# Whole second experts, two or three early down-weight blocks, and the last output columns of the first experts in four pieces

## The reference, cut to what matters

```python
def _ec_moe(h, w_router, w_gate, w_up, w_down):        # first block: 16 experts, 32 tokens each
    cap = EC_FACTOR * L // N_EXPERTS
    vals, idx = lax.top_k(jnp.swapaxes(aff, 1, 2), cap)
    hid = silu(einsum('becd,edf->becf', xs, w_gate)) * einsum('becd,edf->becf', xs, w_up)
    y = einsum('becf,efd->becd', hid, w_down) * vals[..., None]
    return jnp.zeros_like(h).at[bidx, idx].add(y)
# the block ends with x + mod * moe, then _rmsnorm(x, norm_final_g)

def hier_moe(x, ...):                                   # each of the two layers: 4 groups x 8 experts
    g_star = argmax(lg)                                 # one group per token
    top_v, top_i = lax.top_k(le, TOP_K_IN_GROUP)        # two experts of the group per token
    for g in range(N_GROUPS):
        h = silu(einsum('td,edf->tef', t, w_gate[g])) * einsum('td,edf->tef', t, w_up[g])
        y = y + einsum('tef,efd->td', h * gate[:, g, :, None], w_down[g])

def second_block(...):
    for l in range(2):
        mix = hybrid_mixer(x, ...)                      # attention of three kinds
        x = layer_norm(ALPHA * x + mix, ...)
        x = layer_norm(ALPHA * x + hier_moe(x, ...), ...)
```

## Time and profile before

| | us |
|---|---|
| median of 3 runs | 1617.17 (1615.1 to 1618.91) |
| the profiled execution | 1616.84 |
| its span in the trace | 1615.1 |
| TensorE busy | 1344.6 (83%) |
| DMA | 492.62 MB, mean 305 GB/s |
| first experts | about 230 to 701 |
| mixer, layer 0 | about 711 to 923 |
| experts, layer 0 | about 923 to 1151 |
| mixer, layer 1 | about 1159 to 1372 |
| experts, layer 1 | about 1372 to 1601 |

### The profile page before, as it was taken

How to read it: one execution, slowest core, us unless ns; L and a number is a source line. 1 busy time by engine, 2 the same in 40 slices (tenths; PEclk the granted TensorE clock), 3 DMA queues, 4 the chain that set the end, 5 groups by cost and what they waited for, 6 DMA issues and landing times. The chain is left out here.

```text
span 1615.1 us, 18893 instructions
## 1 busy us (share of the span) xinstructions
PE 1344.6 (83%) x7496; PEld 747.6 (46%) x7496; DVE 482.2 (30%) x1128; ACT 297.7 (18%) x617; POOL 0.2 (0%) x4
## 2 busy tenths in 40 slices
PE   6999999956665656599999999866999989998658
PEld 4665877412211211166767743321567677433213
DVE  5125553101101101014664522210246744322102
ACT  2422202100000000012332312200223223122002
POOL 0000000000000000000000000000000000000000
PEclk9999999978878878799999999997999999999889
DMA  9465478999999999992421499999915214899994
GB/s 392 165 253 208 159 292 329 399 428 427 428 428 427 428 428 428 428 425 78 191 105 53 164 396 391 410 409 408 388 53 209 86 71 157 343 401 409 409 407 193
DMA packets 63297, 492.62 MB, mean 305 GB/s; under 512 B 7008, under 2 KB 7392, under 8 KB 39008
## 3 DMA queue, kind: packets, MB, share of 16 engines
q1 hardware_dynamic: 63056, 491.15, 74.9%
q10 hardware_dynamic: 144, 0.13, 0.0%
HBM read 490.21 MB, written 1.05 MB: 304 GB/s over the span
## 5 line engine op out<-in xcount | busy, mean ns | idle before, releaser
L659 PE MATMUL PS<-A 128*128 128x256 f32 (+5 forms) x1568 | 367.5, 392 | 5.3 <-DMA A<-ring_d 1.6
L1015 PE MATMUL PS<-A 128*32 128x512 f32 x1536 | 234.2, 747 | 140.1 <-DMA A<-ring_d 140.1
L659 PEld LDWEIGHTS PS<-A 128*128 128x128 f32 (+1 forms) x1568 | 274.3, 193 | 90.1 <-issue 51.0
L1540 PE MATMUL PS<-A 128*32 128x512 f32 (+1 forms) x1024 | 168.0, 628 | 41.1 <-DMA A<-ranked_d 32.9
L1015 PEld LDWEIGHTS PS<-A 128*32 128x32 f32 x1536 | 52.5, 125 | 308.6 <-issue 239.6
L1569 PE MATMUL PS<-A 128*32 128x512 f32 (+1 forms) x512 | 93.9, 713 | 31.6 <-issue 31.6
L1540 PEld LDWEIGHTS PS<-A 128*32 128x32 f32 (+1 forms) x1024 | 48.1, 123 | 143.9 <-issue 143.3
L2096 DVE TENSOR_TENSOR A<-A,PS 128x512 f32<-128x512 f32 x8 | 5.5, 688 | 322.7 <-PE PS L1015 322.7
L664 PE MATMUL PS<-A 128*128 128x128 f32 (+1 forms) x396 | 58.4, 278 | 18.2 <-DVE A L2096 7.1
L664 PEld LDWEIGHTS PS<-A 128*128 128x128 f32 (+1 forms) x396 | 44.7, 144 | 56.0 <-issue 31.0
L1569 PEld LDWEIGHTS PS<-A 128*32 128x32 f32 (+1 forms) x512 | 25.9, 137 | 96.0 <-issue 95.4
(11 more groups left out here) (392 smaller groups left out, 1277.8 us busy)
## 6 DMA issues: line engine op xcount, KB each, us to landing
A<-ring_d SPq DMA_DIRECT2D x156, 2048.0 KB, 26.3
A<-ranked_d SPq DMA_DIRECT2D x240, 512.0 KB, 14.7
A<-ranked_d SPq DMA_DIRECT2D x24, 1024.0 KB, 8.4
A<-ring_d SPq DMA_DIRECT2D x2, 1312.0 KB, 22.2
A<-ring_d SPq DMA_DIRECT2D x2, 1280.0 KB, 22.4
A<-p_d SPq DMA_DIRECT2D x1, 1232.0 KB, 22.6
A<-xT_d SPq DMA_DIRECT2D x1, 1024.0 KB, 5.3
A<-cT_d SPq DMA_DIRECT2D x1, 1024.0 KB, 11.8
```

Source lines behind the costliest of these rows:

```text
L659: ins = g.matmul(out, l, r, start=n == 0, stop=n == len(pairs) - 1)
L1015: ins = g.matmul(ps[32 * e:32 * e + 32, :], rows_of(kk, e), wv[:, kk % 2, e, :], start=kk == 0, stop=kk == 7)
L1540: ins = g.matmul(ps[m * s:m * s + m, :], XS2[u % 2][:, kk, c:c + m], wv[:, kk % nk, s, :], start=kk == 0, stop=kk == 7)
```

## The change

**1. Whole experts.** A `gr` block is now gate and up of one expert, one DMA of 2 MB; a `dr` block of a unit with four experts holds two experts, 2 DMAs of 1 MB. `gate_up` of units 4 to 10 waits for all of its 2 or 4 blocks, does its matmuls, and frees all slots at its end. SyncE reads the experts' numbers at other places.

**2. Early down blocks.** Three more places for blocks, used once per layer (`ONCE`): slot 12 is `YE2[0]`, a quarter of `XGT` and the arrays `PX2[1]`, `PXG[1]` and `GB1`; slot 13 is half of `XGT` and the place of `YE2[1]`; slot 14 (last layer alone) lies in `Ho` and `ARENA2`. The down blocks of units 0 and 1 (and 2 in the last layer) go there, and are asked for before their turn (`AHEAD`). SyncE waits for the end of the mixer's use of these arrays. The second group's tokens are gathered behind unit 3 instead of units 1 to 3, since they are written where the early blocks lie, and the copy of the first half of `ye2` waits for both halves in units 0 and 1.

**3. The last columns of the first experts.** The last four `w_down` blocks hold 128 columns and all rows each. Each piece is multiplied, copied, combined and squared by itself.

```diff
@@ -92,7 +92,7 @@
     x, j = UNITS[n]
     if x == 0:
-        return [(j // 2 + 1, j % 2)]
+        return [[(1, 0)], [(1, 1)], [], [(2, 0), (2, 1)]][j]
...
-    return {1: (0,), 2: (1,), 4: (0,), 5: (1,)}.get(n, ())
+    return {3: (0, 1), 4: (0,), 5: (1,)}.get(n, ())
...
+AHEAD = [{(2, 1): 0, (3, 1): 1}, {(2, 0): 2, (2, 1): 0, (3, 1): 1}]
...
-IDS_BEHIND = {("gu", 3, 0): range(0, 4), ("gu", 3, 1): range(4, 8), ("dn", 4): range(8, 10)}
+IDS_BEHIND = {("gu", 3, 1): range(0, 2), ("gr", 1, 0, 0): range(2, 4), ("gr", 1, 0, 1): range(4, 6), ("dn", 6): range(6, 10)}
...
-    + [4, 5, 0, 1, 2, LAST_SLOT, 4, 5, 0, 1] + [2, LAST_SLOT, 4, 5, 6, 0, 1] * 6 + [2, LAST_SLOT, 4, 5, 6, 0] \
...
+    + [4, 5, 0, 1, 2, LAST_SLOT, 4, 5, 0, 1] + [2, LAST_SLOT, 4, 5, 6, ONCE, 0, 1, ONCE + 1] + [2, LAST_SLOT, 4, 5, 6, 0, 1] * 5 + [2, LAST_SLOT, 4, 5] \
...
+        RING += [[YE2[0], V(Mo + quarter, quarter), V(behind, half_slot)],
+                 [V(Mo + half_slot, half_slot), V(mem_of_ye1, half_slot)],
+                 [V(Ho, half_slot), V(ARENA2, half_slot)]]
...
+            def last_columns(q):
+
+                w, i = weights("w_down", 3, 1, q)
+                wv = w.rearrange("p (k e n) -> p k e n", k=8, e=4)
+                ps = fresh("ye", 3, 1, q)
+                arrived(i)
+                for kk in range(8):
+                    for e in range(4):
+                        ins = g.matmul(ps[32 * e:32 * e + 32, 0:128], HIDT[:, kk, 32 * e:32 * e + 32], wv[:, kk, e, :], start=kk == 0, stop=kk == 7)
+                ins.then_inc(*full("ye", 3, 1, q))
+                finished(i)
...
+            last_columns(3)
+            squares((6,), 6, "row")
+            keep_on(1, "ye", 3)
+            combine_row(7)
+            keep_on(2, "ex", 3)
+            squares((7,), 7, "row").then_inc(*full("fsum"))
...
+            def whole_experts(n, ps):
+
+                (x, j), u = UNITS[n], gather_of(n)
+                m = 32 if four(n) else 64
+                got = [weights("gr", l, x, j, s) for s in range(128 // m)]
+                wv = [w.rearrange("p (k n) -> p k n", k=8) for w, i in got]
+                for d in range(4):
+                    g.wait_ge(*at("xs2", l, u, d // 2, d % 2))
+                for w, i in got:
+                    arrived(i)
+                for kk in range(8):
+                    for s in range(128 // m):
+                        c = (j % 2) * 128 + s * m
+                        ins = g.matmul(ps[m * s:m * s + m, :], XS2[u % 2][:, kk, c:c + m], wv[s][:, kk, :], start=kk == 0, stop=kk == 7)
+                ins.then_inc(*full("sg", l, n))
+                for w, i in got:
+                    finished(i)
...
-                full("ye2", l, p, 0)
+                full("ye2", l, p, int(p < 2))
...
-                n = SLOT // len(of)
-                c = n * part + (4096 if kind == "dr" else 0)
+                of, n, c = (of[part:part + 1], SLOT, 0) if kind == "gr" else (of[2 * part:2 * part + 2], SLOT // 2, SLOT)
...
+                if SLOTS[i] >= ONCE:
+                    q.wait_ge(*at(*(("full", "pv", key[1], "dil", 3), ("full", "wo", key[1], 3), ("sc", key[1], "dil", 3))[SLOTS[i] - ONCE]))
```

More of the change, by code:

```diff
@@ L1110, in tensor @@
                 g.wait_ge(*at("hidt", x, 1))
-                for half in range(2):
+                for half in range(2 if x < 3 else 1):
                     ps = fresh("ye", x, half)
@@ L1535, in gate_up @@
+                for part in range(2):
+                    if (n, part) in AHEAD[l]:
+                        d = AHEAD[l][n, part]
+                        state["down", d] = weights("dn", l, 2 * d)
+                    w, i = weights("gu", l, n, part)
+                    wv = w.rearrange("p (k s n) -> p k s n", k=4, n=512)
+                    for d in (2 * part, 2 * part + 1):
                         g.wait_ge(*at("xs2", l, u, d // 2, d % 2))
                     arrived(i)
-                    for kk in range(nk * part, nk * part + nk):
-                        for s in range(128 // m):
-                            c = (j % 2) * 128 + s * m
-                            ins = g.matmul(ps[m * s:m * s + m, :], XS2[u % 2][:, kk, c:c + m], wv[:, kk % nk, s, :], start=kk == 0, stop=kk == 7)
@@ L1541, in gate_up @@
-                    ins.then_inc(*(full("sg", l, n) if part == parts_ - 1 else up("pe")))
+                    for kk in range(4 * part, 4 * part + 4):
+                        for s in range(2):
+                            c = (j % 2) * 128 + s * 64
+                            ins = g.matmul(ps[64 * s:64 * s + 64, :], XS2[u % 2][:, kk, c:c + 64], wv[:, kk % 4, s, :], start=kk == 0, stop=kk == 7)
+                    ins.then_inc(*(full("sg", l, n) if part else up("pe")))
+                    finished(i)
@@ L1552, in turned, with down_weights @@
                 turn(ps[:, 256:384], pxg).then_inc(*full("hd", l, p))
+            def down_weights(w):
+                pieces = w if type(w) is list else [w]
+                return [p[:, c:c + SLOT // 4] for p in pieces for c in range(0, p.shape[-1], SLOT // 4)]
             def down(n):
@@ L3293, in sync @@
                     ranked(i, x, *key)
+                elif x >= ONCE:
+                    c = 0
+                    for part in RING[x]:
+                        wide = part.shape[-1]
+                        q.dma_start(part, ring_d[row[i], :, c:c + wide]).then_inc(*land(f"ring{x}", *(("landed", i) if c + wide == n else ())))
+                        c += wide
                 else:
```

98 lines of the change are left out of this document (56 added, 42 removed).

## The result

The changed kernel takes 1611.26 us (median of 20 runs, 1606.06 to 1619.67), the kernel before 1616.98 (20 runs on the same chips, 1613.57 to 1624.11). The ratio is 0.9961, with a 95% interval of 0.9950 to 0.9973: 6.3 us less (4.4 to 8.1). The forecast of 1604 was 13 us less. The direction is right, and less than half of the gain came.

The account below looks back on a forecast made before the run. TensorE bounds each expert stage up to about unit 6, DMA landings from unit 8. Columns -3.2, layer 0 -4.7 and layer 1 -5.1 sum to -13.0 us: 1604 us forecast, range 1597 to 1615.

Parts of the forecast that it names:

- the rate behind it: Expert stage, 27 blocks from unit 4's down block to the last landing: 133.4 us, a gain of about 6.3 per layer.
- rival A: Units 8 to 10: long `gate_up` bursts starve the DMA queue, 10 us more than forecast, 1627 us; chance 10%.
- The lead-in loss: Before unit 6: slots held to `gate_up`'s end make unit 4's down block land 1.7 (layer 0), 2.4 us (layer 1) later.
- my sum: Whole kernel: -3.2 us last columns, -4.7 layer 0, -5.1 layer 1, together -13.0 us.
- Early blocks, nothing: Part 2, before the expert stages: the DMA runs 9.8 and 14.7 us ahead, but slots bind, so nothing is gained.
- The hole about unit 4: Sign that the forecast is right: the DMA idles some 10 us about unit 4 while SyncE waits for `gate_up`.
- Rival B: Expert stages: slots don't bind and the early blocks count in full, giving 1575 us; chance 5%.
- The size of rows: Expert-stage transfers: 16 KB rows move at 428 GB/s against 409, `gr` blocks 4.90 us for 5.13, `dr` blocks 5.0.
- Rival C: Expert-stage transfers: larger rows move no faster when the queue is full, only the columns gain, 1614.5 us; chance 10%.
- The last columns, 3.2 us: Part 3, end of first experts: last landing to root takes 4.2 us for 7.4, and the mixer carries the gain on.
- Bursts: Sign that the forecast is right: bursts of `gate_up` on TensorE take 7 to 10 us.
- the own range: The forecast's own range, 1598 to 1610 us: DMA term -2 to -7 per layer, columns -2 to -4.

Follow-up runs that it names:

- a kernel without held slots: Changed kernel with whole experts only for units 7 to 10, units 4 to 6 in row parts: 1604.18 us; without early blocks 1603.99 us.
- the other order: Changed kernel with each `combine_row` ahead of the next `last_columns`, fewer idle products: 1609.30 us; with whole experts only for units 7 to 10 too: 1603.26 us.
- expert by expert: Changed kernel with each expert's products done one behind another, freeing each slot early: 1706.58 us, 1.0570 of the kernel before; without early blocks 1704.21 us.

## Why the prediction was right or wrong

**The step that failed** is the second of part 1, "the rate behind it: a gain of about 6.3 us per layer". It counted 27 blocks back to back from the landing of unit 4's down block. I had priced held slots at units 4 and 5, and asked whether bursts of units 8 to 10 starve the queue (rival A), where TensorE waits for landings and four free blocks are asked for in time. I didn't ask it of unit 6. This is the first unit of four, it holds four of seven slots, and TensorE isn't waiting there: its `gate_up` starts when TensorE comes to it (1012.14), not when its blocks have landed. So unit 7's third block couldn't be asked for before 1019.4. The term was 6.3 and 6.9 us a layer and measured 3.7 and 3.1 in the trace. Of the 6.4 us that are missing, unit 6's hold is 4.3 (1.7 and 2.6). The rest is mostly one block a layer that was asked for in time and came 1.1 and 1.4 us late, which stays open. With unit 6 in parts alone the 27 blocks take 134.5 / 135.5 us, so 3.2 of the 6.4 come back.

**The lead-in loss** was right in the trace in layer 0 and 0.9 too large in layer 1 (+1.7 and +1.5 us, forecast +1.7 and +2.4). I booked it as a price of the part, so it is no part of the shortfall, but it was avoidable. That units 4 to 6 in parts take 1604.2 us, the very forecast, is luck: that kernel doesn't have the lead-in loss. Without it my sum gives 13.0 + 4.1 = 17.1 us less, 1600, and 15.2 (12.3 to 18.3) were measured.

**Early blocks, nothing:** right, measured alone (0.9994 [0.9983, 1.0005]), beside whole experts (0.9970 with them, 0.9968 without) and in a kernel without held slots (0.9906 with them, 0.9915 without). The hole about unit 4 with SyncE waiting for `gate_up` is there as described. Rival B is out.

**The size of rows:** right as to the rate. Seven slices at 410 to 425, single blocks 4.9 apart, pairs 4.95 for my 5.0, and with four DMAs of 4 KB rows the gain vanishes; that it is the row and not the number of DMAs isn't shown. Rival C is out; the trace of before had the answer, 409 against 428 GB/s.

**The last columns, 3.2 us:** the runs have 3.6 (1.8 to 5.5) alone, and 1.4 on top of the other parts, which their intervals don't tell from none. Both ends of the difference were wrong: before is 7.4 to 9.8 and not 7.4, the new form 6.0 to 9.3 and not 4.2 (5.3 and 6.9 in the other order). The traces show 1.5 us at the root, 0.7 of it at unit 0, where I had let the mixer carry all of it. That the number came out near mine was in part luck. I read a single execution and left TensorE's own readiness out: with the old form its products start with the landing where the length is 7.4, and 2.3 us behind it where it is 9.7 and 9.8.

**Bursts:** 8.4 to 10.0 us, forecast 7 to 10; the last `down` stands at 1149.18 behind a landing at 1149.1, and 1.0 behind in layer 1 (0.6 forecast). Rival A, that bursts behind waits starve the queue, is out: in 1015 to 1140 it moves 418 GB/s. A hold does starve it, at another unit and by another mechanism than a slow clock.

**Slips that change little:** the layer-1 sum takes 7.03 us for a `gate_up` that the earlier trace rows has at 7.09; the terms of the own range (-2 to -7 us a layer, -2 to -4 for the columns) give 1599 to 1611 and not 1598 to 1610; and the earlier trace rows has, beside the 390 to 428 GB/s named for the expert stages, slices at 388 and 343.

## What to carry to other kernels

When a change makes a step take its buffers all at once, walk the ring unit by unit and ask at each whether the consumer starts when the data land or when it comes to them. In the first case the hold was free here, in the second the queue ran dry before the slots came back, 1.7 and 2.6 us for a step of 7.07; so use the large transfers only from the unit on at which the consumer waits. Sum the gain from the last instant at which the queue can be starved, and check which that is after the change, not before. And take a handover of a few microseconds from more than one execution: here the same code gave 7.4 and 9.8, and a mixer in code that is alike 226.1 and 228.4.

## What the runs showed of the hardware

Products of 32 columns overlap when they write different quarters of the output's 128 partitions by turns. The same 64 products of 128 x 512 took 7.07 us by turns on four quarters, 12.25 on two, 22.59 on one, all at a granted clock of 1.00. The Trainium skill (TensorEngine Tiling (Array Packing), Overview) gives up to 4 times, as a theoretical figure, for 32 columns; 22.59 / 7.07 is 3.2. What it costs to reorder such products is seen in expert by expert: 95 us.

A block asked for while another is on its way took longer to land: the third block of unit 7 takes 10.1 us from its issue at 1019.4, where the block ahead of it landed at 1022.97; a lone one takes 7.6. Of two asked for together with nothing on its way, the first took 8.9 in the earlier trace rows, but 7.4 at 988.09 in the changed kernel, so these rows give no rule for that case.
